# A transformer layer on one core: attention branches summed in PSUM from probabilities normalised in place, with split first and last pieces

## The reference

```python
h = x @ w_in                            # 256 x 1024 by 1024 x IN_COLS
# sparse attention, 8 heads of 64 in 2 key groups; three branches of the same queries
s_cmp = q . k_cmp * 64**-0.5            # 15 compressed keys (gelu MLP over blocks of 32 tokens)
s_slc, s_win                            # 256 keys each, causal (window and selection cover all keys here)
o = g0 * softmax(s_cmp) @ v_cmp + g1 * softmax(s_slc) @ v_slc + g2 * softmax(s_win) @ v_win
# gated linear recurrence, 4 heads of 128; RMS norm per head, times silu(g)
x1 = layer_norm(x * alpha + concat(o, o_b) @ w_out)
x2 = layer_norm(x1 * alpha + cross_attention(x1, mem))        # 4 heads of 256
# product-key experts: scores, top 16 of 16384, gelu(down @ t) * gate, @ up
x3 = layer_norm(x2 * alpha + experts(x2))
```

## Time and profile before

| | us |
|---|---|
| runs, median of 3 (lowest, highest) | 1116.79 (1115.67, 1118.95) |
| the profiled execution's own time | 1112.96 |
| its span in the profile | 1110.8 |
| PE busy with matmuls | 1070.3 |
| DVE busy | 766.9 |
| ACT busy | 512.5 |
| mean granted clock of PE, share of full | 0.988 |

### The profile page before, as it was taken

One profiled execution on the slowest core, in us unless ns is written; L12 is line 12 of the kernel. 1 busy time (PEld: TensorE's weight loads), 2 busy tenths in 40 slices (PEclk: granted clock), 3 DMA queues, 4 the chain that ended last, 5 costly groups with the idle time before them and its releaser, 6 DMA issues.

```text
span 1110.8 us, 19015 instructions
## 1 busy us (share of the span) xinstructions
PE 1070.3 (96%) x7742; PEld 971.1 (87%) x7742; DVE 766.9 (69%) x1414; ACT 512.5 (46%) x801; POOL 84.6 (8%) x58
## 2 busy tenths in 40 slices
PE   5999999999899999999999999999999999999995
PEld 5987798779799999999999999988888888888884
DVE  4446666674779987454887876478889885555555
ACT  4355433454445555545444444544444444544451
POOL 3000000000047840000000000000000000000000
PEclk9899999999989999999999999999999999999998
DMA  9652332563414655555454555665555555565561
GB/s 338 243 186 95 96 95 77 166 216 115 152 54 156 190 176 186 185 175 189 156 169 155 169 157 169 188 210 171 171 175 173 172 180 189 191 190 191 191 196 67
DMA packets 50438, 186.65 MB, mean 168 GB/s; under 512 B 5808, under 2 KB 5856, under 8 KB 49840
## 3 DMA queue, kind: packets, MB, share of 16 engines
q1 hardware_dynamic: 48384, 176.71, 49.1%
...
## 4 chain that ended last, share of the span: by engine, by line
PE 88%; DVE 7%; ACT 2%; issue 1%; DMA 1%; SPq 0%; DVEq 0%; ACTq 0%
PE psG L1185 16%; PE psS L1503 16%; PE psT L1503 15%; PE psG L1186 15%; PE psG L1187 15%; PE psO L1487 1%; PE psO L1488 1%; DVE lo L739 1%; ACT hi L551 1%; PE psO L1417 1%; PE psO L1377 1%; DVE x L776 1%; PE psS L1329 1%; DVE x L770 1%; DMA raw<-in_w_stream 1%
## 5 line engine op out<-in xcount | busy, mean ns | idle before, releaser
L739 DVE TENSOR_TENSOR lo<-raw,hi 128x1024 fp32r<-128x1024 f32 x303 | 369.2, 1221 | 207.1 <-ACT hi L551 206.7
L551 ACT ACTIVATE hi<-raw 128x1024 fp32r<-128x1024 f32 x331 | 350.2, 1059 | 286.2 <-DMA raw<-in_up 193.2
L1185 PE MATMUL psG<-b_hi,hi 128*128 128x256 f32 x1152 | 332.3, 288 | 0.7 <-DVE b_lo L1055 0.7
L1186 PE MATMUL psG<-b_lo,hi 128*128 128x256 f32 x1152 | 327.3, 284 | 0.0
L1187 PE MATMUL psG<-b_hi,lo 128*128 128x256 f32 x1152 | 327.2, 284 | 0.0
L1185 PEld LDWEIGHTS psG<-b_hi,hi 128*128 128x128 f32 x1152 | 222.5, 193 | 1.6 <-issue 1.4
L1186 PEld LDWEIGHTS psG<-b_lo,hi 128*128 128x128 f32 x1152 | 222.5, 193 | 0.2
L1187 PEld LDWEIGHTS psG<-b_hi,lo 128*128 128x128 f32 x1152 | 222.4, 193 | 0.0
L1163 DVE TENSOR_TENSOR act_lo<-H,act_hi 128x256 fp32r<-128x256 f32 x128 | 54.0, 423 | 99.0 <-ACT act_hi L723 98.9
L705 ACT ACTIVATE H<-psG 128x256 f32<-128x256 f32 x128 | 49.2, 384 | 152.4 <-PE psG L1187 152.4
L1503 PE MATMUL psS<-hi,act_hi 128*128 128x512 f32 x256 | 81.9, 401 | 0.0
...
## 6 DMA issues: line engine op xcount, KB each, us to landing
raw<-in_down SPq DMA_DIRECT2D x128, 512.0 KB, 3.7
raw<-in_up SPq DMA_DIRECT2D x128, 512.0 KB, 4.2
...
```

The costliest lines, as they stand in the source:

```text
L551: act.activation(hi[n % DEPTH][:], raw[slot(n)][:], ACT.Copy).then_inc(hi_done, 1)
L739: dve.tensor_tensor(lo[slot(n)][:], raw[slot(n)][:], hi[n % DEPTH][:].bitcast(FP32), ALU.subtract)\
L1185: pe.matmul(out, hi_l, hi_r, start=start, stop=False)
L1186: pe.matmul(out, hi_l, lo_r, start=False, stop=False)
```

## The change

Part by part:

- **Start.** `xT` comes in four quarters and the first weight tile in two halves. PE waits for each piece alone. The load of `norm_w` moves behind PE's start.
- **Hidden layer.** `blk` is stationary, padded to 32 columns, and `w1` moves (128 columns). Four partial sums lie on four groups of 32 PSUM partitions (L1448). ACT copies them out, and one more matmul with `pick` (L1453) adds and transposes them.
- **Units.** The order is now by pair of heads: long branches first, then one compressed unit per pair, with both halves of the tokens. A new DVE step `weigh` divides the probabilities by their row sum and applies the gate in place, ahead of the transposes. `values` has the values stationary (64 columns) and the probabilities moving; all five units of a pair add into one PSUM bank, transposed. `gather` (ACT copy, DVE remainder) takes a pair out. `combine`, `o_acc` and the transposes of `o_acc` go. The mask matmul covers 128 keys per head and follows the products. The rows of `w_out` are permuted to match.
- **Order around the units.** `bare` entries are gemms whose `rest` on DVE stands later, as `feed_lo`. The decay of the recurrence runs per head. The last step, j = 7, computes and copies 64x64 corners only. The compressed layer stands behind the second unit's scores.
- **After the units.** `read_out` and RMS norm run per half of the tokens, with tiles between them. The last three `w_out` tiles are run as a joint block, tokens 0 to 127 first, and the norm of the first half runs beside the second. `turn_lo` is an entry of its own. `normalize` works on halves of the width.
- **End.** The last four `up` tiles (`last`) are all added to `psS` first, then to the first 512 columns of `psT`, then to the others. The output leaves in four DMAs.

The diff, cut to its core (in `weigh` the removed lines of `combine` are left out):

```diff
-UNITS = [(b, pair, t) for b in range(2) for pair in range(REP // 2) for t in range(NT)]
+UNITS = []
+for pair in range(REP // 2):
+    UNITS += [(b, pair, t) for b in range(2) for t in range(NT)] + [(2, pair, 0)]
+XU = len(UNITS)
...
-    out.append(("hidden", 0))
+    out += [("hidden", 0), ("scores", 0)]
     gemm(1)
     out.append(("gelu", 0))
     gemm(1)
-    out.append(("compressed", 0))
-
-    last = len(UNITS) + NT - 1
-    out.append(("scores", 0))
+
+    last = XU - 1
     for u in range(last + 1):
-        gemm(2 if u < 2 else 1)
+        out.append(("weigh", u))
+        if u < 2:
+            gemm(1)
+        else:
+            out.append(("feed_lo", n - 1))
+        bare(1)
         if u >= 2:
             out.append(("level", (u - 2, 0)))
         out.append(("turn_probs", u))
-        if u + 1 < last:
+        if u < last:
             out.append(("scores", u + 1))
+        if u == 0:
+            out.append(("compressed", 0))
+        out.append(("feed_lo", n - 1))
         if u in (6, 7):
             out.append(("silu", u - 6))
-        gemm(1)
-        if u == 1:
-            assert n == AT["hv"]
-            out.append(("decay", 0))
+        bare(1)
+        assert u != 1 or n == AT["hv"]
+        if u == 0:
+            out.append(("feed_lo", n - 1))
         if u >= 2:
             out.append(("level", (u - 2, 1)))
         out.append(("values", u))
-        if u + 1 == last:
-            out.append(("scores", last))
+        if UNITS[u][0] == 2:
+            out.append(("gather", UNITS[u][1]))
...
-    out += [("level", (8, 0)), ("read_out", 0), ("read_out", 1), ("rms", 0)]
-    gemm(2)
-    out += [("turn", 0), ("turn", 1)]
+    out += [("level", (8, 0)), ("read_out", 0)]
+    gemm(1)
+    out += [("read_out", 1), ("rms", 0), ("rms", 1)]
+    gemm(1)
+    out += [("turn", 0), ("turn_lo", 0)]
+    gemm(1)
+    out += [("turn", 1), ("turn_lo", 1)]
...
-    gemm(2 * KD // 2)
-    out += [("norm", (0, 0)), ("norm", (0, 1))]
-    gemm(2)
-    out.append(("turn", 2))
-    gemm(1)
-    out.append(("turn", 3))
+    gemm(KD - JOINT)
+    joint = range(n, n + JOINT)
+    n += JOINT
+    out += [("joint", joint[0]), ("norm", (0, 0))] + [("feed", m) for m in joint] + [("feed_lo", m) for m in joint[:2]]
+    late = range(n, n + 4)
+    n += 4
+    out += [("bare", late[0]), ("turn", 2), ("norm", (0, 1)), ("bare", late[1]), ("feed_lo", joint[2]), ("bare", late[2]),
+            ("turn", 3), ("turn_lo", 2), ("feed_lo", late[0]), ("turn_lo", 3), ("bare", late[3])]
+    out += [("feed_lo", m) for m in late[1:]]
...
-        out.append(("up", j))
+        out.append(("up", j) if j < E_TILES - LAST else ("last", j))
...
-            for n in range(ALL):
+            for i in range(4):
+                part = slice(2 * i, 2 * i + 2)
+                sp.dma_start(xT[:, part, :], a["xT"][:, part, :]).then_inc(x_in[i], 16)
+                if i % 2 == 0:
+                    half = slice(i * D // 4, (i + 2) * D // 4)
+                    sp.dma_start(raw[0][:, half], a["w_stream"][0][:, half]).then_inc(first_in[i // 2], 16)
+            for n in range(1, ALL):
...
-                step(dve.scalar_tensor_tensor(out=z, in0=z, scalar=m[:, t, 0:1], in1=gb[:, 0, :],
-                                              op0=ALU.subtract, op1=ALU.mult))
-                dve.wait_ge(std_ready, 2 + w * NT + t)
-                step(dve.reciprocal(rs[:, t, 0:1], sd[:, t, 0:1]))
-                step.wait()
                 for half, ready in ((slice(0, D // 2), half_ready), (slice(D // 2, D), norm_ready)):
+                    step(dve.scalar_tensor_tensor(out=z[:, half], in0=z[:, half], scalar=m[:, t, 0:1], in1=gb[:, 0, half],
+                                                  op0=ALU.subtract, op1=ALU.mult))
+                    if ready is half_ready:
+                        dve.wait_ge(std_ready, 3 + w * NT + t)
+                        step(dve.reciprocal(rs[:, t, 0:1], sd[:, t, 0:1]))
+                    step.wait()
...
+            def weigh(u):
+                b, pair, t, heads, keys = unit(u)
                 dve.wait_ge(exp_done, u + 1)
                 sums = row_sum[:, u % 2, 0:heads]
                 if b == 2:
+                    p3 = probs[:, 0:heads * NC].rearrange("p (h n) -> p h n", n=NC)
+                    step(dve.tensor_reduce(sums, p3, AX.X, ALU.add))
+                    step.wait()
+                else:
+                    p3 = probs[:].rearrange("p (h n) -> p h n", n=S)[:, :, 0:keys]
                 step(dve.reciprocal(coef[:, 0:heads], sums))
                 step.wait()
                 col = {0: 1, 1: 2, 2: 0}[b]
+                mine = gate[:].rearrange("p t (g r c) -> p g t r c", g=G, c=3)[:, :, :, pair * 2:pair * 2 + 2, col]
+                if b == 2:
+                    by = coef[:].rearrange("p (g t j) -> p g t j", g=G, t=NT)
+                    step(dve.tensor_tensor(by, by, mine, ALU.mult))
+                    step.wait()
+                    step(dve.tensor_tensor(by, by, cmp_any[:].unsqueeze(1).unsqueeze(3).broadcast_to([P, G, NT, 2]), ALU.mult))
+                else:
+                    by = coef[:, 0:heads].rearrange("p (g j) -> p g j", g=G)
+                    step(dve.tensor_tensor(by, by, mine[:, :, t, :], ALU.mult))
                 step.wait()
+                dve.tensor_tensor(p3, p3, coef[:, 0:heads].unsqueeze(2).broadcast_to([P, heads, keys]), ALU.mult)\
+                    .then_inc(weighed, 1)
...
+            def gather(p):
+                dve.wait_ge(pair_hi, p + 1)
+                high, low = pair_of(p)
+                dve.tensor_tensor(low, psO[:, 0:512].rearrange("p (j n) -> p j n", n=S), high.bitcast(FP32), ALU.subtract)\
+                    .then_inc(pair_lo, 1)
...
+                    if j == 7:
+                        dve.tensor_copy(att[0:64, :, t, 64:P], psM[0:64, :].rearrange("p (n t) -> p n t", t=P)[:, :, 64:P])\
+                            .then_inc(level_merged, 1)
...
-                for group in range(G):
-                    both = psS[:, group * 512:(group + 1) * 512].rearrange("p (j n) -> p j n", n=S)
-                    pe.matmul(both[:, :, 0:keys], identb[:],
-                              causal[:, S - keys:S].unsqueeze(1).broadcast_to([P, 2, keys]), start=True, stop=False)
                 for j in range(2):
                     for group in range(G):
                         at = (group * 2 + j) * S
-                        mm = pe.matmul(psS[:, at:at + keys], qT[group * HD:(group + 1) * HD, 2 * g + j, t * P:(t + 1) * P],
-                                       kT[b][group * HD:(group + 1) * HD, 0:keys], start=False, stop=j == 1)
+                        pe.matmul(psS[:, at:at + keys], qT[group * HD:(group + 1) * HD, 2 * g + j, t * P:(t + 1) * P],
+                                  kT[b][group * HD:(group + 1) * HD, 0:keys], start=j == 0, stop=False)
+                for group in range(G):
+                    both = psS[:, group * 512:(group + 1) * 512].rearrange("p (j n) -> p j n", n=S)
+                    mm = pe.matmul(both[:, :, keys - P:keys], identb[:], causal[:].unsqueeze(1).broadcast_to([P, 2, P]),
+                                   start=False, stop=True)
...
-                if u:
-                    pe.wait_ge(combined, u)
+                first = u % (XU // 2) == 0
+                if first and g:
+                    pe.wait_ge(pair_lo, g)
+                acc = psO[:, 0:512].rearrange("p (j n) -> p j n", n=S)
                 if b == 2:
-                    for h in range(NH):
-                        gg = h // REP
-                        mm = pe.matmul(psO[:, h * HD:(h + 1) * HD], probsT[0:NC, h * P:(h + 1) * P],
-                                       vcmp[:, gg * HD:(gg + 1) * HD], start=True, stop=True)
+                    for group in range(G):
+                        rows = slice(group * HD, (group + 1) * HD)
+                        mm = pe.matmul(acc[rows].rearrange("p j (t n) -> p t j n", t=NT), vcmp[:, rows],
+                                       probsT[0:NC, group * 512:(group + 1) * 512].rearrange("p (t j n) -> p t j n", t=NT, j=2),
+                                       start=False, stop=True)
                 else:
-                    for r in range(REP):
-                        for kb in range(t + 1):
-                            at = (r * (t + 1) + kb) * P
-                            mm = pe.matmul(psO[:, r * HD:(r + 1) * HD], probsT[:, at:at + P],
-                                           vg[:, kb, b * P + r // 2 * HD:b * P + (r // 2 + 1) * HD],
-                                           start=kb == 0, stop=kb == t)
+                    for kb in range(t + 1):
+                        for group in range(G):
+                            rows = slice(group * HD, (group + 1) * HD)
+                            both = probsT[:, 0:heads * (t + 1) * P].rearrange("p (g j k n) -> p g j k n", g=G, j=2, n=P)
```

(31 more changed lines are left out.)

346 lines of the change are left out of this document (184 added, 162 removed).

## The result

The changed kernel takes 1084.89 us (median of 4 runs, 1083.90 to 1085.98), the kernel before 1117.39 us beside it (4 runs, 1115.67 to 1118.95). The ratio is 0.971, with a 95% interval of 0.9692 to 0.9728. The profiled execution took 1085.98 us, its span is 1083.8; against the profiled execution of before (1112.96) that is 27.0 us less. So 1086.5 was forecast for a median of 1084.89. The forecast gain was 30.2 us; the profiled executions show 27.0, the medians 32.5.

A forecast was written before the change was run, and what follows sets the result against it. PE, busy 1070.3 us, was taken to set the pace, so only matmul time or PE's waits could be saved. Terms summed to 30.2 us: 1116.8 - 30.2 = 1086.6, rounded to a median of 1086.5; range 1079 to 1100.

The forecast's parts named there:

- Start: Up to the second weight tile: loading and rounding in quarters and halves lets PE begin sooner, 3.0 us, bounds 1.5 and 4.5.
- Hidden layer: The layer's 64 records: four column groups side by side take 1.9 us instead of 8.11, saving 6.2 us.
- the clock behind it: Behind the hidden layer: clock at 0.71 of full for 8 us stays full once thin matmuls go, 2.3 us.
- Values: Products of probabilities and values in all units: two column groups side by side give 0.63, 1.07 and 1.07 us, saving 5.4.
- Other matmuls: Mask 0.9, compressed scores 1.2, corners at j = 7 0.6, fewer transposes 0.9, added `pick` -0.3: 3.3 us saved.
- Recurrence: Recurrence levels: `bare` puts copies ahead of remainders, removing 2.2 us of PE's 2.7 us waits for factors.
- `weigh`: DVE step between exp and transposes: costs PE 0 us, hidden with a thin margin of 0.2 us.
- Read-out, turns, `w_out`: Between the units and `w_out`: 0 us gained, with 2 to 3 us of PE waits as before.
- Norms: First norm's wait for `o_lo` shrinks from 2.3 to 0.3 us, gaining 2.0; second norm's halves cost 0.3.
- End: Last four tiles and the work behind them: `psS` complete earlier, so the last output comes sooner, 3.1 us.
- column groups that don't overlap: Rival on hidden layer and values: 5.0 and 6.9 us more, time 1098.5 to 1101; chance 0.12.
- a late DVE queue: Rival on the ten units: each waits 1 us for `weigh`, and the level behind it too, 1096.5; chance 0.12.

## Why the prediction was right, and where it was not

**Start (3.0 us): the step is right, the gain is not there.** PE's second tile begins at 13.5 us, not at 12.8; before it was 15.7, so the pieces bring 2.2 us. The wait behind `blocks` (3.26 us, where PE waited 0.56 before) and 1.7 us of half clock take back 4.4. What the prediction left out is what the moved start does to POOL's queue and DVE's: `w1`'s load hangs on the third remainder, `kcp` behind it lands 1.0 to 3.2 us later than before (31.8 to 34.0 us in the profiles, 30.8 before), DVE waits for it in `blocks` with a weight tile's remainder behind. In the kernel before DVE waited 2.1 us there, and PE's wait in that place was one of 0.56 us for `qT`. The prediction counted the load of `norm_w` as one that moves away from the front, and did not name that it moves in front of `w1`; the run on that alone doesn't settle its share. The run with the old start shows that the pieces gain nothing in this kernel as it stands. What stands behind the start on DVE had no term in the sum; that is the step that failed.

**Hidden layer (6.2) and the clock behind it (2.3): right.** 8.11 becomes 1.88 us, 6.2, and undoing it costs 8.25 us where the two terms give 8.5. The working had 8.11 us as the price of the old form; 1.1 of them were half clock, so the four groups gave 5.1 and the clock 1.1 + 2.3. That the clock fell from thin matmuls is shown as far as their form goes: it falls with 30 columns moving past 128 of weights and not with 128 past 32.

**Compressed layer (1.3): right**, the wait for `hz` is gone.

**Values (5.4): right.** 0.58, 1.01 and 1.00 us, where 0.63, 1.07 and 1.07 were worked out. That two groups overlap as the four do is read from the durations; no run undid it for `values` alone.

**Other matmuls (3.3): about 1 us too small.** Scores and mask of a unit take 0.80 and 1.22 us from first matmul to the next product, where they took 0.96 and 1.59, so 4 x 0.16 + 4 x 0.37 = 2.1 us instead of the 0.9 for the mask; the compressed scores 1.00 instead of 1.47, so 0.9 instead of 1.2.

**Recurrence (2.2): too small.** The waits of the levels sum to 3.7 us from 89 to 147 us of the kernel before, and none over 0.3 us is left. The prediction took two groups of the waits, and left 0.5 of them in place. The run with the remainders in front confirms the cause.

**`weigh` (0): right, with the wrong margin.** No wait for `probs` is left. The margin is 0.75 to 2.0 us, not 0.2. The chain from the second level's end was taken with everything queued in front of it; in the trace DVE has idle time of 1.1 us and more within each unit, so it is done earlier. The run with longer `weigh` shows that the measured margin is the one that decides.

**Read-out, turns, `w_out` (0): right in its waits.** 0.87 for `oh`, 0.90 and 1.01 us for `o_lo`, 2.8 in all, where 2 to 3 were expected; before there were 3.2. But the last of them, 1.01, stands behind the first matmul of `w_out`, so of the 3.2 us only 1.8 are left in the stretch ahead of it. That gives 1.4 of its 2.5 us; 0.9 are the shorter turns (counted among the other matmuls), and 0.2 stay open.

**Norms (2.0 - 0.3): 1.8 us too large.** PE's wait at the first norm is 0.73 us, not 0.3; and the last of the waits for `o_lo`, 1.0 us, falls into `w_out` itself, which leaves 0.4 of the 2.0 in that stretch. The second costs 0.5 us more than before, where 0.3 was expected. The half clock behind it is from standing still, as the run with the filled waits shows.

**End (3.1): right in its mechanism.** `psS` is complete 5.5 us ahead of the last matmul, and the end follows 14.6 us later. PE waited 0.36 us, not 0.7, for the fourth tile's remainder. Behind the last matmul the gain is 4.3 us, with the 0.4 of that wait given back in the tables. The working had 3.5 + 0.2 behind the last matmul, less 0.6 for the wait; with `LAST = 1` the trace takes 3.4 us more, so most of it is shown by a run as well.

**Clock at 168 us (1.7): right**, it is full there.

The rivals: column groups that don't overlap are excluded, a late DVE queue in the units too (though the real late queue stood at `blocks`), and the ends paid only at one end. The number of the rival with DVE's late queue was too low for its own words: ten waits of 1 us alone make 1096.5, and the waits of the levels were to come on top.

**The total: partly luck.** By stretches the changed kernel lacks 4.9 us at the start, 1.6 from `w_out` on, 0.2 at the second norm and 0.9 in the tables, and has 1.7 us more than forecast in the units, 1.6 in the turns and 1.2 at the end. That is some 3.1 us too little, as the profiled executions show: 1085.98 us, where 1082.8 was forecast. For the median the forecast added 3.8 us, the distance of the kernel before's median from its profiled execution. The changed kernel has no such distance; its profiled execution is 1.1 us above its median. So the median came out 1.6 us better than forecast although the sum was 3.1 us too high: two errors against each other.

The runs of the kernel before say what the distance is. Beside the later experiments its executions with a granted clock of 0.987 or 0.988, like the profiled one's 0.988, take 1111.95 to 1113.19 us, those with 0.982 or 0.983 take 1116.96 to 1119.17. The median of 1116.8 us lies with the latter; five thousandths of 1113 us are 5.6 us. The changed kernel's four runs are at 0.991 to 0.995. So by the medians the change also won back clock that the one trace of the kernel before doesn't show as lost. Where in the kernel that clock was lost, no trace here shows.
